# Moving VectorE's rotation, rope sum and weight cast behind the low half of the turned weights in a decoder layer kernel

## What is computed

```
proj = einsum('bsd,de->bse', x, w_in)                 # q, k, v, gates

# stick-breaking attention, 8 heads, in blocks of 128 queries
z = q @ k.T * scale
log_beta, log_1m_beta = log_sigmoid(z), where(mask, log_sigmoid(-z), 0)
suffix = reverse_cumsum(log_1m_beta) - log_1m_beta
a = where(mask, exp(log_beta + suffix), 0)
out = a @ v

# differential attention, 4 heads, on rotated q and k
rope(x) = concat([x1 * cos - x2 * sin, x2 * cos + x1 * sin])
w = softmax(z1) - lam * softmax(z2)
```

## Time and profile before

| | us |
|---|---|
| median of 3 runs | 1491.87 (1490.63 to 1493.86) |
| the profiled execution, device time | 1491.23 |
| its span, first to last instruction | 1489.3 |
| TensorE busy | 1468.7 (99%) |
| VectorE busy | 989.1 (66%) |
| ScalarE busy | 665.7 (45%) |
| GpSimd busy | 356.8 (24%) |

### The profile page before, as it was taken

How to read it: one execution, slowest core, us unless ns; L and a number is a source line. 1 busy time by engine, 2 the same in 40 slices (tenths; PEclk the granted TensorE clock), 3 DMA queues, 4 the chain that set the end, 5 groups by cost and what they waited for, 6 DMA issues and landing times. The chain is left out here.

```text
span 1489.3 us, 19461 instructions
## 1 busy us (share of the span) xinstructions
PE 1468.7 (99%) x7188; PEld 1223.4 (82%) x7188; DVE 989.1 (66%) x1236; ACT 665.7 (45%) x1037; POOL 356.8 (24%) x280
## 2 busy tenths in 40 slices
PE   9999999999999999999999999999999999999997
PEld 8788888887888887888888888888888888888886
DVE  3676776768857456454366788766664477668767
ACT  3455554556556555452032244444443534433343
POOL 2635445355444233311240040000000000000004
PEclk9999999999999999999999999999999999999999
DMA  5101112111111101111451225544442688836563
GB/s 180 58 29 57 57 43 70 57 56 44 57 36 50 29 15 42 29 43 58 141 212 62 91 89 183 184 156 156 156 148 93 225 294 271 308 132 194 190 200 134
DMA packets 111648, 172.41 MB, mean 116 GB/s; under 512 B 6096, under 2 KB 71888, under 8 KB 111440
## 3 DMA queue, kind: packets, MB, share of 16 engines
q1 hardware_dynamic: 111568, 171.33, 33.8%
HBM read 127.27 MB, written 44.04 MB: 115 GB/s over the span
## 5 line engine op out<-in xcount | busy, mean ns | idle before, releaser
L759 PE MATMUL p_proj<-xt_h,w_hi 128*128 128x512 f32 x640 | 254.0, 397 | 0.6 <-DVE xt_l L1608 0.6
L763 PE MATMUL p_proj<-xt_h,w_lo 128*128 128x512 f32 x640 | 252.7, 395 | 0.0
L761 PE MATMUL p_proj<-xt_l,w_hi 128*128 128x512 f32 x640 | 251.2, 392 | 0.0
L2307 POOL TENSOR_TENSOR w_lo<-w_raw,w_hi 128x512 fp32r<-128x512 f32 x96 | 133.6, 1412 | 210.1 <-DVE w_hi L1616 209.6
L2426 POOL TENSOR_TENSOR row_odd<-row_odd,gains 128x1024 f32<-128x1024 f32 x4 | 10.4, 2615 | 578.4 <-ACT row_odd L1580 578.4
L763 PEld LDWEIGHTS p_proj<-xt_h,w_lo 128*128 128x128 f32 x640 | 120.3, 188 | 23.7
L759 PEld LDWEIGHTS p_proj<-xt_h,w_hi 128*128 128x128 f32 x640 | 120.4, 188 | 22.7 <-DVE xt_l L1608 0.6
L761 PEld LDWEIGHTS p_proj<-xt_l,w_hi 128*128 128x128 f32 x640 | 120.5, 188 | 20.7
L1608 DVE TENSOR_TENSOR d_al<-f_a,d_ah 128x1024 fp32r<-128x1024 f32 x56 | 68.5, 1224 | 75.0 <-ACT d_ah L1497 74.9
L1497 ACT ACTIVATE d_ah<-f_a 128x1024 fp32r<-128x1024 f32 x56 | 59.2, 1057 | 129.5 <-PE p_av L1149 54.9
L1349 ACT ACTIVATE a_t<-p_tr 128x384 fp32r<-128x384 f32 (+3 forms) x96 | 47.2, 491 | 123.5 <-PE p_tr L861 123.4
(11 more groups left out here) (297 smaller groups left out, 3527.2 us busy)
## 6 DMA issues: line engine op xcount, KB each, us to landing
f_a<-h_terms SPq DMA_DIRECT2D x56, 512.0 KB, 3.4
w_raw<-w_in SPq DMA_DIRECT2D x40, 512.0 KB, 3.9
h_terms<-c SPq DMA_DIRECT2D x40, 512.0 KB, 3.1
f_b<-w_ff SPq DMA_DIRECT2D x40, 512.0 KB, 4.9
r<-w_ff SPq DMA_DIRECT2D x32, 512.0 KB, 4.0
gate_rows<-gst SPq DMA_DIRECT2D x12, 512.0 KB, 5.0
y<-x SPq DMA_DIRECT2D x8, 512.0 KB, 8.0
wo_raw<-w_out SPq DMA_DIRECT2D x8, 512.0 KB, 10.0
```

Source lines behind the costliest of these rows:

```text
L759: pe.matmul(o, w_hi[n_slot][:, k, :], xt_h[:, k, cols], start=(k == 0), stop=False)
L761: pe.matmul(o, w_hi[n_slot][:, k, :], xt_l[:, k, cols], start=False, stop=False)
L763: mm = pe.matmul(o, w_lo[n_slot][:, k, :], xt_h[:, k, cols], start=False, stop=(k == KT - 1))
L2307: low = pool.tensor_tensor(w_lo[slot][:, ks, :], w_raw[:, ks, :], w_hi[slot][:, ks, :].bitcast(F32), ALU.subtract)
```

## The change

In stick-breaking groups the rotation, the rope sum and the cast leave the end of a step and come in the next step, behind the sub and `out_low`, ahead of the product and the scans. The rope sum of a half comes in the step behind its rotation, as before. Differential groups keep their order, TensorE, ScalarE, GpSimd and SyncE keep theirs in all groups, and no instruction or wait is added or dropped.

```
                         if b == 0 and u > 0:
                             out_low(u - 1)
+                        due, to_turn = to_turn, []
+                        if to_sum:
+                            rope_sum(*to_sum.pop())
+                        for half in due:
+                            rope_half(*half)
+                            to_sum.append(half)
+                        if tile_due is not None:
+                            split_next(tile_due)
                         if b == 0 and u + 2 < G.nunits:
                             product(u + 2)
...
-                    if to_sum:
+                    if to_sum and not G.sb:
                         rope_sum(*to_sum.pop())
...
                     for i in G.halves_at(k):
-                        if G.is_rope(i // 2):
+                        if G.is_rope(i // 2) and G.sb:
+                            to_turn.append((i // 2, i % 2))
+                        elif G.is_rope(i // 2):
                             rope_half(i // 2, i % 2)
                             to_sum.append((i // 2, i % 2))
                     tile_due = tile_after(G, k)
-                    if G.sb and tile_due is not None:
-                        split_next(tile_due)
-                if not G.sb and tile_due is not None:
+                if tile_due is not None:
                     split_next(tile_due)
```

More of the change, by code:

```diff
@@ L1765, in attention @@
                         combine(u)
-                to_sum, tile_due = [], None
+                to_sum, to_turn, tile_due = [], [], None
                 if G.is_rope(0):
```

## The result

| | median, us | runs |
|---|---|---|
| before | 1491.68 (1490.63 to 1493.86) | 7 |
| changed | 1497.36 (1496.91 to 1497.67) | 7 |

The ratio is 1.0037, with a 95% interval of 1.0027 to 1.0047: the change makes the kernel slower by 5.7 us, or 0.4%. The span of the profiled execution went from 1489.3 to 1494.9 us. Forecast were 1501.5 us and a range of 1490 to 1505.

A forecast was written before the change was run, and what follows sets the result against it. TensorE, busy 1468.7 of 1489.3 us, bounds the kernel, so only its waits count. Groups 0 to 2 lose 4.2 us and group 3 5.4, together +9.6 on 1491.87: 1501.5 us, range 1490 to 1505.

The forecast's parts named there:

- turns 17 and 18: Each of groups 0 to 3: turn 17 gains 0.4 us, turn 18 loses 0.65, `values` 0.3; +0.9 us a group.
- the queue of step 6: VectorE from the sub of step 6 to that of step 7: 7.25 us in group 3, 6.65 in groups 0 to 2.
- the late copies of step 3: Group 3: ScalarE's copies into `swap` start at 358.0, not 356.95, behind a later rope sum.
- What can be won: Only TensorE's waits for the sub, at turn 17 of four groups and turns 1 to 4 of group 3: some 6 us.
- The price of the cast: GpSimd's `w_lo` (2.54 us) follows the cast and now falls between product and scans in full; the sub isn't held up.
- Turns 0 to 10 of group 3: Turns 3 and 4 come 0.4 to 0.6 us earlier, turn 8 loses 3.2; +4.2 us in all (2 to 5).
- The 0.9 of turn 9 and the 0.3 behind it: Group 3: GpSimd's mask and product delay rope sum and scans of unit 10; turn 9 loses 0.9 us, its `values` 0.3.
- The other casts: Step 6 of groups 0 to 2 and step 10 of all four: 0.2 us each a group; step 20: 0.1; step 2: nothing.
- The first: Rival: waits go and nothing replaces them; turn 17 gains up to 0.8 us, turns 3 to 5 about 1.5; 1487 us; chance 0.11.
- the second: Rival: gains and losses cancel; turn 8 of group 3 loses 1 us, turn 17 nets nothing; 1492 us; chance 0.14.
- The third: Rival: lag reaches the next place, unit 14's mask late in all groups; 2.5 us a group, 7 in group 3; 1506 us; chance 0.13.
- What would show it: Turn 17 without wait, turn 18 waiting; group 3's turns 8 and 9 waiting longest (2.5, 0.9 us), its window about 5 us longer.

The follow-up runs named there:

- the twins: Kernel before and changed kernel, each with GpSimd's low half made for one of eight k-slices only in stick-breaking groups: 1488.08 and 1490.47 us.
- The last combined version: Kernel before with GpSimd's low half one step later and, in group 3, rope sum, rotation and casts reordered, including the cast ahead of the steps: 1486.88 us.

## Why the prediction was right, and where its sizes were off

The sign and the places were right, and so was the mechanism at turns 17 and 18 and in the queue of step 6. The size was not: 5.7 us came of 9.6 forecast. Two errors of opposite sign lie in it, so that it came as near as it did is in part luck: turn 22 cost 2.0 us in sum where 0.4 was forecast, and all other terms together 3.8 where 9.2 was. One link of the chain, the late copies of step 3, did not happen. Point by point:

- **What can be won.** Right: only turns that wait for the sub matter. The last combined version is 5.1 us ahead at the start of group 4, of the some 6 us that I had counted. GpSimd's later low half gives 2.4 of them, in all four groups; the other 2.7 come from VectorE's order and the casts in group 3.
- **The price of the cast.** Right, and shown by the twins: `w_lo`, which runs between the scans, is what costs at turn 18 and in turns 1 to 10 of group 3. That the sub isn't held up holds too (0.66 us at 118.44, with the second `w_lo` beside it). The rule of the Trainium skill ("SBUF — State Buffer", section "Who interferes with whom"), by which the one that comes second is blocked for the whole instruction, agrees with these rows: the long scan took 2.93 us for 2.08, the pair of `w_lo` 4.30 for 2.54.
- **Turns 17 and 18.** Forecast +0.9 us a group; from turn 16 to 21 the lag grew by 0.30, 0.14, 0.20 and 0.30. The gain at turn 17 was forecast as 0.4 and is 0.44 to 0.54. Turn 18 was put 0.65 us behind the kernel before and came 0.1 to 0.3 behind: the sub of step 17 was expected to start at 123.95 and did at 123.4 on the old scale (123.18 and 0.22). `values` behind turn 19 was to lose 0.3 and lost under 0.1. The "1.7 us behind" of the prediction doesn't follow from its own times, which put that sub 2.2 us behind (123.95 for 121.79); it was 1.6.
- **Turns 0 to 10 of group 3.** Forecast +4.2 (its parts, 3.2, 0.9 and 0.3, add up to 4.4), it is +2.8. Against the start of the group, turn 2 lost 0.25 (forecast up to 0.4), turn 3 gained 0.45 (0.4), turn 4 1.17 (0.6), and turn 8 came at +1.6 (+3.2). The 0.9 of turn 9 and the 0.3 behind it are 0.82 and 0.40. What failed first is the start of ScalarE's copies of step 3: on the old scale they started at 356.9 (358.73, less 2.07 of lag and plus 0.22), no later than before, and not at 358.0. The queue of step 2 ahead of them is 5.6 us (351.70 to 357.32); by the terms of the list for step 6, with the shorter product and scan of this step, it would be about 6.2 (an estimate). The copies of step 5 did come late, by 1.5 us against the group (367.44 for 364.08), and the sub of step 6 by 0.3: 368.65 on the old scale, where it was at 368.33 and I had it at 369.8. The queue of step 6 is 6.72 us for 7.25.
- **The other casts.** Steps 6 and 10: forecast 0.2 each a group, measured nothing. In group 0 the queue of step 6 is 6.12 us for 6.65. Step 20: forecast 0.1 and at most 0.3, measured 0.4 to 0.5 in each of four groups. This term named the place and GpSimd's low keys but priced neither: the first subtraction behind the cast took 2.20 us, where it had taken 1.21.
- **Sum.** Groups 0 to 2: forecast 4.2, measured 2.07. Group 3: forecast 5.4, measured 3.7. One term fails in nearly all places: the queue in which VectorE and GpSimd take turns came out 0.53 us too long in step 6 of group 0 and in step 6 of group 3. The starts show where: product, first `w_lo` and short scan are 2.28 us (372.88 to 375.16) for 2.25, but the second `w_lo` and the long scan 2.06 (375.16 to 377.22) for 2.53. The rest is the cast, 0.6 for 0.7.
- **The share of the rope sum.** The prediction did not part cast and rope sum. Alone rotation and rope sum cost 1.9 us in group 3 and the cast 0.4, together 2.8, so for 0.5 us they need each other.
- **Rivals.** The first (a gain, no lasting loss) was not met, and would have needed more than `w_lo` elsewhere: with the low half a step later the changed order still takes 1494.6 us, and only with `w_lo` cut short is it faster than the kernel before, 1490.5. Parts of the second came true. Its condition, copies within 0.3 us of their old time, was met in step 3 (0.1 us sooner), the sub of step 6 came within 0.3 us of its old time, and turns 17 and 18 net 0.1 to 0.3 us. What it lacked is the long queue behind that sub (turn 8 lost 1.6 us and not 1), turns 9 and 10 (1.2 us) and turn 22 (2.0). The third was not met; what was left of VectorE's lag at step 10 did not reach step 14.
- **What would show it.** At turns 17 and 18 every sign came. Turn 8 of group 3 has the longest wait (1.86 us, not 2.5), but turn 18 (0.85) comes ahead of turn 9 (0.64). Group 3 is 3.7 us longer and not 5, groups 0 to 2 are 0.6 to 0.8 each and not 1 to 2.

What stays open: why the second `w_lo` and the long scan take 0.5 us less than their own lengths add up to. That their records overlap is argued, no run measures it. Why the first subtraction of step 20 takes 1.21 us beside the low keys in one order and 2.20 in the other is not taken apart either.

## What to carry to other kernels

An instruction that releases work on another engine is priced with that work: in turns 1 to 10 of group 3 the moved cast of 0.7 us cost nothing by itself (the twins differ by 0.07 us), but the 2.5 us that it started on GpSimd then ran beside VectorE's scans rather than beside its idle time. Before bringing an instruction nearer to those who wait for it, look at what else is released and what it holds up. Here leaving VectorE's order alone and moving GpSimd's background work behind its urgent work won 2.4 us, and moving VectorE's work instead lost 5.7. An instruction that runs beside the other engine's work can also cost by its place alone, as the cast at turn 22 did (2.0 us). In a strict queue, also ask whether the job that is put back is itself ahead of something: the rope sum, which nobody on TensorE waits for, started ScalarE's copies and, where it was put, stood ahead of the scans; its place cost 2 us.

## What the runs showed of the hardware

VectorE's instructions with two inputs in SBUF, its casts, and GpSimd's subtractions, products and masks take turns in these traces, whole instruction by instruction, and a waiting one goes ahead of the other engine's next: a scan of 128 columns took 0.42, 0.68 or 1.51 us, a cast of a weight tile 0.68 or 1.47, a pair of `w_lo` 2.54, 3.18 (a short scan in between) or 4.30 (a long one). The next instruction in VectorE's own queue went ahead of the one on GpSimd that the previous one released: the scan at 115.14 took its 0.42 us, and `w_lo` is recorded from 115.30. Held-up time is recorded as busy: VectorE's busy time rose from 989.1 to 994.1 us and GpSimd's from 356.8 to 365.5 with not an instruction more. Unexpected was how exactly this repeats: on the same path, lags of the changed kernel and of its variants agree to 0.05 us over 24 turns. Behind one wait of 2.12 us TensorE's granted clock was 0.50 of full speed for some 3.4 us, in one execution; behind a wait of 1.86 us it stayed at 1.00, in two (the changed kernel, and the one with the last cast in place).
